# A projection's second pass with the rows of tiles 3 and 4 ahead of the old taps, and other moved steps

## The chip, the cores and the metric

The kernel runs on one NeuronCore of a Trainium2 chip. A core has five engines that take their instructions in order and meet by semaphores: TensorE (PE, matrix products), VectorE (DVE), ScalarE (ACT), GpSimd (POOL) and SyncE (SP), which here issues most of the DMAs. The metric is the device time of one execution in microseconds.

## The reference

One encoder layer, run on a prompt of 256 tokens and a sample of 2048, 2304 rows of 1024 channels in all, with the same weights. Cut to what matters:

```python
xn = rms_norm(x, norm1)
proj = xn @ w_in                       # hyena x0, x1, v | q | k | v
y_hy = hyena_mixer(...)                # short conv on x0, x1, v, then x0 * (filter * (x1 * v)) with an FFT
y_at = window_gqa(...)                 # |q - k| <= 128, q and k normed per head
h = x + concat(rms_norm(y_hy), rms_norm(y_at)) @ w_out
y = h + (silu(gate) * up) @ w_down     # gate, up = rms_norm(h, norm2) @ w_gate_up
```

All of it is fp32. A product of fp32 accuracy is made of three matmuls in a rounded fp32 format: each operand is split into a high part (a cast on ScalarE) and a low part (operand less high part, on VectorE), and high x high, low x high and high x low are summed. The function `triple` (lines 83 to 87) issues the three, so most of TensorE's rows carry the lines 85, 86 and 87.

## The kernel before

The program has three parts: `front` (input projection, the filter network and the long convolution's first half), `mixers` (convolution's end, attention, output projection) and `swiglu`. The change lies in `front` and at the seam of the other two.

`front` handles 18 tiles of 128 tokens, in 6 rounds over three groups of 6 tiles (`GT = 6`, `NG = 3`). Rounds 0 to 2 are the first pass, with 8 units each (the hyena's v and x1 columns). Rounds 3 to 5 are the second pass, with 10 units each (x0, q, k, v); there the rows come back from a copy in DRAM. A unit is 128 columns of `w_in`, and has two runs, c = 0 and c = 1, each over half of the group's tokens. A run is 24 matmuls, in two halves of 12 (`first_half`, `second_half`). Run 0 needs tiles 0 to 3 of the group, run 1 also tiles 4 and 5 (and, where the group "peeks", the first row of the next one, `turn(r, 6)`).

What each name does to the engines:

- `norm(n)`: the row sums of tile n on ScalarE (lines 1153 and 1155, the latter with another table of functions), the scaling on VectorE (1425). It belongs to the first pass.
- `turn(r, j)`: tile j of the round is transposed by TensorE (924, first pass) or read back (second pass), cast to `pr_xhi` in two halves by ScalarE (1188) and split to `pr_xlo` in two halves by VectorE (1451). VectorE counts the semaphore `x_low` by two per tile, and TensorE's runs wait for it. SP saves the tile before (559) and loads one ahead (551) in the same step.
- `weights(n)`: high and low part of a unit's weights (1161, 1429).
- `evict(r, i, c)`: the taps of the short convolution of a finished run: centre tap on ScalarE (1230), the two others on VectorE (1471, 1473), for the first pass followed by a product on GpSimd (761).
- the generator `side` holds the other work: the filter network with its sines (ScalarE 1280, 1292; VectorE 1518; GpSimd's preparation 767 to 772), the filter's transform in eighths (VectorE 1558, 1572), the transform of u (1346, 1576), and the products with the filter (TensorE's `pr_gen`, VectorE 1609, GpSimd 849 and 850, ScalarE casts, VectorE 1592 and 1596) and the return steps with the input `ir_z` (ScalarE 1396). `woven` advances it by one step at each `yield` of `course`.

`course` is one schedule that is run once per engine, with the engine's own pieces. So where it puts a call ahead of another, this holds on every engine that has a piece for it. On the way from one round to the next it has `turn(r, 2)`, the eviction of the last run, a side step, `turn(r, 3)`, a norm and a side step, ahead of unit 0. The second pass's scaling needs none of the norms, so there the norm is empty.

At the seam, the mixers' last tile t = 17 on GpSimd takes the low part of the hyena output, then that of the attention output (1974), then adds squares in pairs (1980, 1982), which TensorE sums with a matmul of ones (`am_score`, 2126). `scale_row(t)` scales the output row of a tile; the last two are called `close(0)` and `close(1)` and are handed to `swiglu`, whose GpSimd part calls them ahead of its first sums.

## Time and profile before

| | us |
|---|---|
| median of three runs | 2855.79 |
| lowest, highest | 2845.22, 2858.62 |
| profiled execution, its own time | 2853.9 |
| its span from the first to the last instruction | 2852.1 |
| PE busy | 2751.9 (96%) |
| DVE busy | 1869.4 (66%) |
| ACT busy | 1224.9 (43%) |
| POOL busy | 1031.1 (36%) |
| mean granted clock of TensorE | 0.991 |

A row of a timeline gives the start in us from the beginning of the span, the length, the engine (PE TensorE, DVE VectorE, ACT ScalarE, POOL GpSimd, SPq SyncE's queue), the line, the operation with output and inputs, and in brackets the idle time of that engine just ahead of it with what released it. `x4` says that four such instructions stand in a row; the length is then that of all four together. The granted clock is 1.00 at TensorE's full rate of 2.4 GHz and 0.50 at its lower level of 1.2 GHz.

### The profile page before, as it was taken

How to read it: one execution, taken by the hardware profiler on the slowest of the kernel's cores; microseconds unless marked ns; L12 is line 12 of the kernel's file. 1: busy time of each engine (PE TensorE's matmuls, PEld its weight loads, DVE VectorE, ACT ScalarE, POOL GpSimd, SP SyncE). 2: the span in 40 equal slices, each digit the busy share in tenths (PEclk: the TensorE clock that was granted, in tenths of full speed). 3: DMA queues.
4: the chain of work that ended last, by engine and by line, in shares of the span. 5: the costliest groups of instructions: out<-in, count | busy, mean ns of one | idle time of the engine just before them, and what ended most of it. 6: DMA issues, size and time to landing. Idle time of an engine off the chain costs nothing.

```text
span 2852.1 us, 38291 instructions
## 1 busy us (share of the span) xinstructions
PE 2751.9 (96%) x14280; PEld 2493.0 (87%) x14280; DVE 1869.4 (66%) x2575; ACT 1224.9 (43%) x1939; POOL 1031.1 (36%) x887
## 2 busy tenths in 40 slices
PE   6988899999998999998999999999999999999999
...
GB/s 207 129 263 176 282 256 235 266 239 174 225 266 211 105 140 127 118 114 180 86 96 102 88 81 71 234 73 92 86 93 78 78 195 105 64 78 67 71 67 67
DMA packets 391553, 405.30 MB, mean 142 GB/s; under 512 B 46271, under 2 KB 327231, under 8 KB 391080
## 3 DMA queue, kind: packets, MB, share of 16 engines
...
## 4 chain that ended last, share of the span: by engine, by line
PE 88%; DVE 5%; DMA 3%; issue 2%; ACT 2%; POOL 1%; SPq 0%; DVEq 0%; POOLq 0%; ACTq 0%
PE ff_banks L85 11%; PE ff_banks L87 11%; PE ff_banks L86 11%; PE ff_down L85 7%; PE ff_down L86 6%; PE ff_down L87 6%; PE pr_acc L85 4%; PE pr_acc L86 4%; PE pr_acc L87 4%; PE pr_gen L85 3%; PE pr_gen L87 3%; PE pr_gen L86 3%; PE am_mix L85 2%; PE am_mix L86 2%; PE am_mix L87 2%
## 5 line engine op out<-in xcount | busy, mean ns | idle before, releaser
L2756 POOL TENSOR_TENSOR ff_alo_raw<-ff_alo_raw,ff_silu 128x384 f32<-128x384 f32 x132 | 197.8, 1498 | 695.9 <-DVE ff_alo_raw L2980 622.1
L3002 DVE TENSOR_TENSOR ff_h<-ff_h,ff_down 128x512 f32<-128x512 f32 x396 | 264.5, 684 | 158.6 <-PE ff_down L87 155.7
L85 PE MATMUL pr_acc<-pr_xhi,pr_whi 128*128 128x386 f32 (+1 forms) x864 | 307.6, 356 | 20.1 <-DVE pr_xlo L1451 20.1
L85 PE MATMUL ff_banks<-ff_xhi,ff_ghi 128*128 128x384 f32 x924 | 313.0, 339 | 7.9 <-DVE ff_glo L2990 3.8
L85 PE MATMUL ff_down<-ff_dhi,ff_ahi 128*128 128x512 f32 x792 | 313.0, 395 | 3.5 <-issue 3.5
L86 PE MATMUL ff_down<-ff_dlo,ff_ahi 128*128 128x512 f32 x792 | 313.0, 395 | 0.0
L87 PE MATMUL ff_down<-ff_dhi,ff_alo 128*128 128x512 f32 x792 | 312.8, 395 | 0.0
L85 PE MATMUL ff_banks<-ff_xhi,ff_uhi 128*128 128x384 f32 x924 | 310.7, 336 | 1.1 <-DVE ff_ulo L2990 1.0
L87 PE MATMUL ff_banks<-ff_xhi,ff_glo 128*128 128x384 f32 x924 | 311.4, 337 | 0.0
L86 PE MATMUL ff_banks<-ff_xlo,ff_uhi 128*128 128x384 f32 x924 | 311.1, 337 | 0.0
L87 PE MATMUL ff_banks<-ff_xhi,ff_ulo 128*128 128x384 f32 x924 | 310.0, 336 | 0.0
L86 PE MATMUL ff_banks<-ff_xlo,ff_ghi 128*128 128x384 f32 x924 | 309.9, 335 | 0.0
L86 PE MATMUL pr_acc<-pr_xlo,pr_whi 128*128 128x386 f32 (+1 forms) x864 | 298.4, 345 | 0.0
L87 PE MATMUL pr_acc<-pr_xhi,pr_wlo 128*128 128x386 f32 (+1 forms) x864 | 297.2, 344 | 0.0
L2854 ACT CAST ff_ahi<-ff_alo_raw 128x384 fp32r<-128x384 f32 x132 | 67.8, 514 | 397.4 <-POOL ff_alo_raw L2756 397.2
L85 PEld LDWEIGHTS pr_acc<-pr_xhi,pr_whi 128*128 128x128 f32 x864 | 167.6, 194 | 32.0 <-DVE pr_xlo L1451 22.9
L85 PEld LDWEIGHTS ff_down<-ff_dhi,ff_ahi 128*128 128x128 f32 x792 | 148.5, 187 | 39.3 <-issue 4.4
L85 PEld LDWEIGHTS ff_banks<-ff_xhi,ff_ghi 128*128 128x128 f32 x924 | 173.4, 188 | 10.2 <-DVE ff_glo L2990 4.8
L87 PEld LDWEIGHTS ff_down<-ff_dhi,ff_alo 128*128 128x128 f32 x792 | 148.4, 187 | 36.3
L86 PEld LDWEIGHTS ff_down<-ff_dlo,ff_ahi 128*128 128x128 f32 x792 | 148.5, 188 | 34.6
L85 PEld LDWEIGHTS ff_banks<-ff_xhi,ff_uhi 128*128 128x128 f32 x924 | 173.4, 188 | 3.4 <-DVE ff_ulo L2990 2.0
L86 PEld LDWEIGHTS ff_banks<-ff_xlo,ff_uhi 128*128 128x128 f32 x924 | 173.4, 188 | 1.4
...
## 6 DMA issues: line engine op xcount, KB each, us to landing
...
```

The costliest lines, as they stand in the source:

```text
L85: pe.matmul(out, still[0], moving[0], start=start, stop=False)
L86: pe.matmul(out, still[0], moving[1], start=False, stop=False)
L87: return pe.matmul(out, still[1], moving[0], start=False, stop=stop)
L2756: pool.tensor_tensor(block(prod, c), block(prod, c), silu[c][:], ALU.mult).then_inc(tempered, 1)
L2854: act.copy(block(ahi, c), block(prod, c)).then_inc(a_high, 1)
L3002: dve.tensor_tensor(h[j][:, o], h[j][:, o], down(v), ALU.add).then_inc(added, 1)
```

## The change

Six things move; no instruction of arithmetic is added or taken away.

1. At the start `weights(0)` comes after `turn(0, 1)`. The 13 DMAs of constants on SP are issued in `turn(0, 1)`, behind the first tile's save, where before they came ahead of all turns. GpSimd's preparation of the third filter layer, which needs them, also waits for `x_low` 8.
2. In round 0, `turn(0, 3)` comes ahead of `norm(4)`, and in the first pass the norms of units 1 to 4 come behind the first half of run 1 instead of behind run 0's eviction, with a side step between the two places.
3. In the second pass `turn(r, 3)` comes ahead of the eviction of the last run. The two side steps between the rounds go: one behind run 0 of unit 0, the other behind the first half of run 1.
4. In unit 0 TensorE waits for a count of `x_low` that is one less (the first half of the last tile is enough) ahead of a run's first half, and for the full count ahead of the second half.
5. For the last tile, GpSimd's sums of squares come ahead of the low part of the attention output.
6. `scale_row(16)` is called in the mixers' last round, ahead of that round's store, not by `swiglu`.

```diff
@@ -241,3 +241,2 @@
         norm(1)
-        weights(0)
         turn(0, 0)
@@ -245,2 +244,3 @@
         turn(0, 1)
+        weights(0)
         norm(3)
@@ -249,10 +249,14 @@
             turn(r, 2)
+            if r >= NG:
+                turn(r, 3)
             if r:
                 evict(r - 1, units_of(r - 1) - 1, 1)
+            if 0 < r < NG:
                 yield
-            else:
+            if r < NG:
+                turn(r, 3)
+            if r == 0:
                 norm(GT - 2)
-            turn(r, 3)
             norm(GT * r + GT - 1)
-            if r:
+            if 0 < r < NG:
                 yield
@@ -276,4 +280,2 @@
                     turn(r, 6)
-                if 1 <= i <= 4 and r < ROUNDS - 1:
-                    norm(GT * r + GT + i)
                 if i == end and r < ROUNDS - 1:
@@ -281,2 +283,4 @@
                 yield
+                if i == 0 and r >= NG:
+                    yield
                 now[0] = event(r, i, 1)
@@ -284,2 +288,6 @@
                 first_half(r, i, 1)
+                if i == 0 and r >= NG:
+                    yield
+                if 1 <= i <= 4 and r < ROUNDS - 1:
+                    norm(GT * r + GT + i)
                 if i == end and r < ROUNDS - 1:
@@ -571,2 +579,11 @@
 
+        def constants():
+            for dst, src in ((cw[:], conv), (gq[:], gains), (ones[:], block_ones)):
+                sp.dma_start(dst, src).then_inc(consts, 16)
+            for dst, src in ((zt[:], z), (w1[:], f_w1), (w2[:], f_w2), (cols[:], f_cols), (w3in[0:64, 0], f_w3[:, 0:HY]),
+                             (w3in[0:64, 1], f_w3[:, HY:2 * HY]), (w3in[64:128, 1], f_w3[:, HY:2 * HY])):
+                sp.dma_start(dst, src).then_inc(f_consts, 16)
+            for s in range(2):
+                sp.dma_start(dec[:, s, :], decay[s]).then_inc(dec_in[s], 16)
+
         def turn(rd, j):
@@ -574,2 +591,4 @@
                 save_x(rd, j - 1)
+            if rd == 0 and j == 1:
+                constants()
             if 2 <= j < GT:
@@ -740,9 +759,2 @@
         bring_w(1)
-        for dst, src in ((cw[:], conv), (gq[:], gains), (ones[:], block_ones)):
-            sp.dma_start(dst, src).then_inc(consts, 16)
-        for dst, src in ((zt[:], z), (w1[:], f_w1), (w2[:], f_w2), (cols[:], f_cols), (w3in[0:64, 0], f_w3[:, 0:HY]),
-                         (w3in[0:64, 1], f_w3[:, HY:2 * HY]), (w3in[64:128, 1], f_w3[:, HY:2 * HY])):
-            sp.dma_start(dst, src).then_inc(f_consts, 16)
-        for s in range(2):
-            sp.dma_start(dec[:, s, :], decay[s]).then_inc(dec_in[s], 16)
         now = [0]
@@ -766,2 +778,3 @@
                     pool.wait_ge(f_consts, 16 * 7)
+                    pool.wait_ge(x_low, 8)
                     pool.tensor_tensor(w3[0:64, 0, :], w3in[0:64, 0, :], w3in[0:64, 1, :], ALU.add).then_inc(w3_sum, 1)
@@ -964,2 +977,5 @@
 
+        def rows_needed(rd, c):
+            return 2 * turn_number(rd, 4 if c == 0 else GT + peeks(rd))
+
         def half_chunk(rd, i, c, ks):
@@ -974,3 +990,3 @@
             if i == 0:
-                pe.wait_ge(x_low, 2 * turn_number(rd, 4 if c == 0 else GT + peeks(rd)))
+                pe.wait_ge(x_low, rows_needed(rd, c) - 1)
                 if rd and c == 0:
@@ -988,2 +1004,4 @@
         def second_half(rd, i, c):
+            if i == 0:
+                pe.wait_ge(x_low, rows_needed(rd, c))
             half_chunk(rd, i, c, range(4, KT)).then_inc(unit_done, 1)
@@ -1973,4 +1991,4 @@
                 pool.wait_ge(mixed, 4 * t - 4)
-            pool.tensor_tensor(ylo[:, t % 2, CT:KT], ao[:, t % 2], yhi[:, t % 2, CT:KT].bitcast(F32), ALU.subtract).then_inc(ya_low, 1)
-            pool.wait_ge(ya_low, t + 1)
+            if t < NTT - 1:
+                attention_rest(t)
             pool.wait_ge(squared, 2 * t + 2)
@@ -1983,2 +2001,8 @@
             pool.wait_ge(gathered, t + 1)
+            if t == NTT - 1:
+                attention_rest(t)
+
+        def attention_rest(t):
+            pool.tensor_tensor(ylo[:, t % 2, CT:KT], ao[:, t % 2], yhi[:, t % 2, CT:KT].bitcast(F32), ALU.subtract).then_inc(ya_low, 1)
+            pool.wait_ge(ya_low, t + 1)
 
@@ -2002,4 +2026,4 @@
 
-        def close(part):
-            scale_row(NTT - 2 + part)
+        def close():
+            scale_row(NTT - 1)
 
@@ -2016,3 +2040,3 @@
                 for i in range(units(n)):
-                    if i == 1 and 3 <= n <= NB:
+                    if i == 1 and 3 <= n:
                         scale_row(n - 3)
@@ -2763,3 +2787,2 @@
         def main(close):
-            close(0)
             sums(1)
@@ -2772,3 +2795,3 @@
                 if q == 0:
-                    close(1)
+                    close()
                 for n, b in enumerate((C11, C22, C21, C12)):
```

How this moves instructions is seen in the order of each engine. First VectorE at the change into group 3 (`pr_xlo` rows of tiles, 128x386 and 128x384 the taps, `fs_` the filter's transform), before:

```order
L1451 TENSOR_TENSOR pr_xlo<-pr_xs,pr_xhi 128x4x128 [waits pr_x_high] x4
L1471 SCALAR_TENSOR_TENSOR pr_cx<-pr_acc,pr_cw,pr_cx 128x386 [waits pr_centred]
L1473 SCALAR_TENSOR_TENSOR pr_cx<-pr_acc,pr_cw,pr_cx 128x386 [waits pr_tapped]
L1558 TENSOR_TENSOR fs_alo<-fs_a,fs_ahi 128x1024 [waits fi_a_high]
L1451 TENSOR_TENSOR pr_xlo<-pr_xs,pr_xhi 128x4x128 [waits pr_x_high] x2
L1558 TENSOR_TENSOR fs_alo<-fs_a,fs_ahi 128x1024 [waits fi_a_high]
L1572 COPY fs_out<-pr_gen 128x512 [waits fi_k_stored1,fi_eighths]
L1429 TENSOR_TENSOR pr_wlo<-pr_raw,pr_whi 128x1024 [waits pr_w_high]
L1451 TENSOR_TENSOR pr_xlo<-pr_xs,pr_xhi 128x4x128 [waits pr_x_high] x4
L1471 SCALAR_TENSOR_TENSOR pr_cx<-pr_acc,pr_cw,pr_cx 128x384 [waits pr_centred]
L1473 SCALAR_TENSOR_TENSOR pr_cx<-pr_acc,pr_cw,pr_cx 128x384 [waits pr_tapped]
L1451 TENSOR_TENSOR pr_xlo<-pr_xs,pr_xhi 128x4 [waits pr_x_high] x2
```

and after:

```order
L1469 TENSOR_TENSOR pr_xlo<-pr_xs,pr_xhi 128x4x128 [waits pr_x_high] x6
L1489 SCALAR_TENSOR_TENSOR pr_cx<-pr_acc,pr_cw,pr_cx 128x386 [waits pr_centred]
L1491 SCALAR_TENSOR_TENSOR pr_cx<-pr_acc,pr_cw,pr_cx 128x386 [waits pr_tapped]
L1447 TENSOR_TENSOR pr_wlo<-pr_raw,pr_whi 128x1024 [waits pr_w_high]
L1469 TENSOR_TENSOR pr_xlo<-pr_xs,pr_xhi 128x4x128 [waits pr_x_high] x2
L1576 TENSOR_TENSOR fs_alo<-fs_a,fs_ahi 128x1024 [waits fi_a_high]
L1469 TENSOR_TENSOR pr_xlo<-pr_xs,pr_xhi 128x4x128 [waits pr_x_high] x2
L1489 SCALAR_TENSOR_TENSOR pr_cx<-pr_acc,pr_cw,pr_cx 128x384 [waits pr_centred]
L1491 SCALAR_TENSOR_TENSOR pr_cx<-pr_acc,pr_cw,pr_cx 128x384 [waits pr_tapped]
L1469 TENSOR_TENSOR pr_xlo<-pr_xs,pr_xhi 128x4 [waits pr_x_high] x2
L1576 TENSOR_TENSOR fs_alo<-fs_a,fs_ahi 128x1024 [waits fi_a_high]
L1590 COPY fs_out<-pr_gen 128x512 [waits fi_k_stored1,fi_eighths]
```

Tile 3's two rows now stand with those of tiles 1 and 2 ahead of the taps, and the filter's low parts and the copy stand behind the weight's low part.

VectorE at the change into group 4 (`sp_pa`, `sp_pb` are the first products with the filter's transform), before:

```order
L1451 TENSOR_TENSOR pr_xlo<-pr_xs,pr_xhi 128x4x128 [waits pr_x_high] x2
L1471 SCALAR_TENSOR_TENSOR pr_cx<-pr_acc,pr_cw,pr_cx 128x384 [waits pr_centred]
L1473 SCALAR_TENSOR_TENSOR pr_cx<-pr_acc,pr_cw,pr_cx 128x384 [waits pr_tapped]
L1451 TENSOR_TENSOR pr_xlo<-pr_xs,pr_xhi 128x4x128 [waits pr_x_high] x2
L1609 TENSOR_TENSOR sp_pa<-sp_k,pr_gen 128x1024 [waits hy_h_spectral,hy_hk_in0]
L1609 TENSOR_TENSOR sp_pb<-sp_k,pr_gen 128x1024 [waits hy_h_spectral]
L1429 TENSOR_TENSOR pr_wlo<-pr_raw,pr_whi 128x1024 [waits pr_w_high]
L1451 TENSOR_TENSOR pr_xlo<-pr_xs,pr_xhi 128x4x128 [waits pr_x_high] x4
L1471 SCALAR_TENSOR_TENSOR pr_cx<-pr_acc,pr_cw,pr_cx 128x384 [waits pr_centred]
L1473 SCALAR_TENSOR_TENSOR pr_cx<-pr_acc,pr_cw,pr_cx 128x384 [waits pr_tapped]
L1451 TENSOR_TENSOR pr_xlo<-pr_xs,pr_xhi 128x4 [waits pr_x_high] x2
L1596 TENSOR_TENSOR sp_ylo<-sp_yf,sp_yhi 128x1024 [waits hy_y_high]
```

and after:

```order
L1469 TENSOR_TENSOR pr_xlo<-pr_xs,pr_xhi 128x4x128 [waits pr_x_high] x4
L1489 SCALAR_TENSOR_TENSOR pr_cx<-pr_acc,pr_cw,pr_cx 128x384 [waits pr_centred]
L1491 SCALAR_TENSOR_TENSOR pr_cx<-pr_acc,pr_cw,pr_cx 128x384 [waits pr_tapped]
L1447 TENSOR_TENSOR pr_wlo<-pr_raw,pr_whi 128x1024 [waits pr_w_high]
L1469 TENSOR_TENSOR pr_xlo<-pr_xs,pr_xhi 128x4x128 [waits pr_x_high] x4
L1489 SCALAR_TENSOR_TENSOR pr_cx<-pr_acc,pr_cw,pr_cx 128x384 [waits pr_centred]
L1491 SCALAR_TENSOR_TENSOR pr_cx<-pr_acc,pr_cw,pr_cx 128x384 [waits pr_tapped]
L1469 TENSOR_TENSOR pr_xlo<-pr_xs,pr_xhi 128x4 [waits pr_x_high] x2
L1627 TENSOR_TENSOR sp_pa<-sp_k,pr_gen 128x1024 [waits hy_h_spectral,hy_hk_in0]
L1627 TENSOR_TENSOR sp_pb<-sp_k,pr_gen 128x1024 [waits hy_h_spectral]
L1614 TENSOR_TENSOR sp_ylo<-sp_yf,sp_yhi 128x1024 [waits hy_y_high]
L1610 TENSOR_TENSOR sp_alo<-sp_a,sp_ahi 128x1024 [waits hy_ha_high]
```

The first pair of products went from ahead of the weight's low part to behind all rows of tiles 4 and 5 and the taps of run 0, next to the first low parts of `sp_y`.

ScalarE in round 0, unit 1 (`fi_feat` is the sine of the filter network, `pr_junk` the row sums of a norm), before:

```order
L1230 ACTIVATE pr_cx<-pr_acc,pr_cw 128x384 [waits pr_u_turned,pr_unit_done]
L1153 ACTIVATE pr_junk,pr_stat<-pr_xs 128x1024 [waits pr_scaled,pr_summed,pr_x_in4]
L1155 ACT_TABLE_LOAD
L1155 ACTIVATE pr_stat<-pr_stat,pr_eps 128x1 [waits pr_summed]
L1280 ACT_TABLE_LOAD
L1280 ACTIVATE fi_feat<-fi_arg 64x1152 [waits fi_wrapped0]
L1284 COPY fi_feat<-fi_feat 64x1 [waits fi_feat_zero,fi_waved]
L1292 CAST fi_fhi<-fi_feat 128x128 [waits fi_feat_first]
L1230 ACTIVATE pr_cx<-pr_acc,pr_cw 128x384 [waits pr_u_turned,pr_unit_done]
```

and after:

```order
L1248 ACTIVATE pr_cx<-pr_acc,pr_cw 128x384 [waits pr_u_turned,pr_unit_done]
L1298 ACTIVATE fi_feat<-fi_arg 64x1152 [waits fi_wrapped0]
L1302 COPY fi_feat<-fi_feat 64x1 [waits fi_feat_zero,fi_waved]
L1310 CAST fi_fhi<-fi_feat 128x128 [waits fi_feat_first]
L1171 ACTIVATE pr_junk,pr_stat<-pr_xs 128x1024 [waits pr_scaled,pr_summed,pr_x_in4]
L1173 ACT_TABLE_LOAD
L1173 ACTIVATE pr_stat<-pr_stat,pr_eps 128x1 [waits pr_summed]
L1248 ACTIVATE pr_cx<-pr_acc,pr_cw 128x384 [waits pr_u_turned,pr_unit_done]
```

The sine now stands ahead of the norm, and one load of a table is gone from between them.

## Rows read from the trace of the kernel before

**Rows 1.** The page's first part: engine busy us, share of the span, instructions.
```profile
PE 2751.9 (96%) x14280; PEld 2493.0 (87%) x14280; DVE 1869.4 (66%) x2575; ACT 1224.9 (43%) x1939; POOL 1031.1 (36%) x887
```

**Rows 2.** The waits of PE: engine, tile, line, releaser: us, times, longest.
```profile
PE pr_acc L85 <- DVE pr_xlo L1451: 20.1, 9, 4.4
```

**Rows 3.** Windows: us, busy by engine, granted clock, DMA share, GB/s.
```profile
433.00:443.00 10.00, 9.24 (x35) 8.71 (x36) 7.22 (x13) 4.32 (x10) 0.53 (x1) 0.69 1.12 342
...
566.00:581.00 15.00, 12.95 (x66) 11.58 (x66) 12.60 (x15) 4.45 (x7) 6.91 (x5) 1.00 1.10 323
```

**Rows 4.** Timelines into group 3: us, length, engine, line, operation, [idle before <- releaser].
```profile
426.39 2.48 DVE L1451 TENSOR_TENSOR pr_xlo<-pr_xs,pr_xhi 128x512 fp32r<-128x512 f32 x4
...
431.10 2.10 DVE L1451 TENSOR_TENSOR pr_xlo<-pr_xs,pr_xhi 128x512 fp32r<-128x512 f32 x2
...
433.25 0.69 PE L85 MATMUL pr_acc<-pr_xhi,pr_whi 128*128 128x386 f32 x1 [3.90 <-DVE pr_xlo L1451]
...
440.32 0.39 PE L85 MATMUL pr_gen<-fs_ahi,pr_g 128*128 128x512 f32 x1
...
442.70 0.44 PE L85 MATMUL pr_acc<-pr_xhi,pr_whi 128*128 128x386 f32 x1 [0.50 <-DVE pr_xlo L1451]
```

**Rows 5.** Timelines of ScalarE, VectorE and TensorE, change into group 4.
```profile
558.60 0.62 ACT L1346 CAST ur_uhi<-ur_us 128x512 fp32r<-128x512 f32 x1 [2.45 <-DMA ur_us<-u_rows]
...
566.85 4.69 DVE L1451 TENSOR_TENSOR pr_xlo<-pr_xs,pr_xhi 128x512 fp32r<-128x512 f32 x4
...
576.18 1.22 DVE L1609 TENSOR_TENSOR sp_pb<-sp_k,pr_gen 128x1024 f32<-128x1024 f32 x1
...
560.05 0.47 PE L85 MATMUL pr_gen<-ur_uhi,ur_ptable 128*128 128x512 f32 x1 [2.18 <-DVE ur_ulo L1576]
...
563.59 0.45 PE L85 MATMUL pr_acc<-pr_xhi,pr_whi 128*128 128x386 f32 x1 [0.56 <-DVE pr_xlo L1451]
...
567.95 0.39 PE L85 MATMUL pr_gen<-ur_uhi,ur_ptable 128*128 128x512 f32 x1
...
572.92 0.45 PE L85 MATMUL pr_acc<-pr_xhi,pr_whi 128*128 128x386 f32 x1 [2.05 <-DVE pr_xlo L1451]
...
577.25 0.39 PE L85 MATMUL pr_gen<-sp_ahi,pr_g 128*128 128x512 f32 x1
...
587.01 0.39 PE L85 MATMUL pr_gen<-sp_ahi,pr_g 128*128 128x512 f32 x1
```

**Rows 6.** Timelines of TensorE and ScalarE, change into group 5.
```profile
758.84 0.69 PE L85 MATMUL pr_acc<-pr_xhi,pr_whi 128*128 128x386 f32 x1 [4.44 <-DVE pr_xlo L1451]
...
765.29 0.40 PE L85 MATMUL pr_gen<-ir_zhi,ir_table 128*128 128x512 f32 x1
...
761.78 1.05 ACT L1396 CAST ir_zhi<-ir_z 128x1024 fp32r<-128x1024 f32 x1 [2.62 <-DMA ir_z<-z_dram]
```

**Rows 7.** Timelines of VectorE, GpSimd, TensorE and ScalarE at the start.
```profile
25.15 2.76 DVE L1451 TENSOR_TENSOR pr_xlo<-pr_xs,pr_xhi 128x512 fp32r<-128x512 f32 x2
...
24.11 2.23 POOL L768 TENSOR_TENSOR fi_h<-fi_w3in 64x512 f32<-64x512 f32 x1
...
27.97 0.69 PE L85 MATMUL pr_acc<-pr_xhi,pr_whi 128*128 128x386 f32 x1 [4.25 <-DVE pr_xlo L1451]
...
29.83 1.06 ACT L1153 ACTIVATE pr_junk<-pr_xs 128x1024 bf16<-128x1024 f32 x1 [4.27 <-DMA pr_xs<-x]
```

**Rows 8.** Timelines of ScalarE and TensorE in round 0, unit 1.
```profile
87.85 1.28 ACT L1280 ACT_TABLE_LOAD   x1
...
92.34 0.76 PE L85 MATMUL pr_gen<-fi_w3hi,fi_fhi 128*128 128x512 f32 x1 [3.62 <-DVE fi_flo L1518]
```

**Rows 9.** Timelines of GpSimd and TensorE at the mixers' last tile.
```profile
1289.83 3.35 POOL L1974 TENSOR_TENSOR am_ylo<-am_ao,am_yhi 128x512 fp32r<-128x512 f32 x1
...
1293.25 1.26 POOL L1980 TENSOR_TENSOR am_sq<-am_sq 128x512 f32<-128x512 f32 x1
...
1295.37 0.61 PE L2126 MATMUL am_score<-am_ones,am_sq 128*128 128x1 f32 x4 [3.74 <-POOL am_sq L1982]
```

## The prediction

> **What bounds the kernel now.** I read the shares of busy time first. TensorE is busy 2751.9 us of a span of 2852.1 [rows 1], so only 100.2 us of the span can be won by moving work, and the change takes no matmul away. Next I read what TensorE waits for: the largest releaser is VectorE's low part of the transposed rows, 20.1 us in 9 waits [rows 2], one or two at each group's start, and there the change works. Then I laid the timelines of TensorE, VectorE, ScalarE and GpSimd side by side at those starts, and at last the granted clock in windows around them. The clock matters as much as the idle time: the window 433 to 443, right behind a wait of 3.90, was granted 0.69, and the window 566 to 581, where the longest wait is 2.05, 1.00 [rows 3, 4, 5]. A run of 24 matmuls takes 440.32 - 433.25 = 7.07 us behind the long wait, 765.29 - 758.84 = 6.45 behind another of 4.44, and 567.95 - 563.59 = 4.36 where no long one precedes [rows 4 to 6]. So a long wait costs itself and up to 2.7 us more, for a stretch at the lower of the two clock levels, 1.2 GHz instead of 2.4.
>
> The profiled run took 2853.9 us (span 2852.1 and 1.8 around it), 1.9 under the median of the three runs, 2855.79, which reach from 2845.22 to 2858.62. My sum starts from 2853.9. About 0.5%, 14.3 us, is what a measurement of this kernel can tell from no change, and the three runs alone span 13.4.
>
> **Start.** Three edits meet: the low part of weight 0 goes behind the rows of tiles 0 and 1, the constants' 13 DMAs go behind the first saved tile, and with them GpSimd's five w3 operations (they now wait for the rows of tile 3). VectorE's pair for tile 3 took 2.76 us at 25.15, while GpSimd added at 24.11 for 2.23 [rows 7]; alone a pair is half of the 2.48 that four took at 426.39, so 1.24 [rows 4]. That is 1.5 us on the wait of TensorE that ends at 27.97 [rows 7]. The first run now starts on the first half of tile 3, one operation of 0.62 earlier, and the weight's low part (1.22 for that size, [rows 5]) is off VectorE's way ahead of it; ScalarE's chain of casts has no slack there and takes part of both back. Of 1.5 + 0.62 + 1.22 = 3.3 I keep 2.8: the first run starts at 25.2. On SP, tile 5's load stands behind a save that stood behind the constants, and its norm waited 4.27 us for it until 29.83 [rows 7]; 13 issues go from ahead of that load's save, so it comes earlier, by an estimated 4 us. Bounds: 1.5 (only the collision goes) to 4 (1.2 of tile 5's lead is kept in the second run as well). **+2.8**.
>
> **Round 0, norm order.** A norm stood ahead of the filter's sine on ScalarE, with a table loaded for it and another back, at 87.85 for 1.28; TensorE waited 3.62 for the filter's low part until 92.34 [rows 8]. With the norm behind the sine, its 1.06 (the same operation in [rows 7]), some 0.5 of small ones and two loads of 1.28 leave the path: the sine is 4.1 earlier. TensorE is ready at 92.34 - 3.62 = 88.7 and VectorE has taps to do first, so I take 89.5: 2.8 earlier. The next eviction on ScalarE and VectorE is then behind the norm, and gives about 1.1 back (an estimate: one norm operation); 1.7 is left, and 0.5 for the clock. Bounds 0 (it all comes back at the next eviction) to 5 (a shorter wait leaves the clock up; a half-rate stretch costs 2.7). **+2.2**.
>
> **Group 3.** Before, taps and the side step's filter work stood on VectorE between the pair of tile 2 (the last of the four from 426.39 for 2.48) and that of tile 3, which began at 431.10 and took 2.10 beside GpSimd's gate [rows 4]. Now six operations run straight from 426.39 at 0.62 each: the first half of tile 3 is ready at 426.39 + 5 x 0.62 = 429.5, and TensorE starts at 429.55 in place of 433.25, 3.7 earlier. But the 12 filter matmuls that filled TensorE between the two tiles are now behind the first run; such a step is 572.92 - 2.05 - 567.95 = 2.92 [rows 5]. Of the 3.7, 2.9 is given back later. The second run's wait of 0.50 at 442.70 goes [rows 4], and the wait of 3.90 becomes one of about 2.95, behind which I count half of a half-rate stretch's 2.7 (1.3) as won, less 0.3 for ScalarE's casts. 3.7 - 2.9 + 0.5 + 1.3 - 0.3 = **+2.3**, bounds 1.1 (clock as before, low taps late) to 3.8 (the whole half-rate stretch gone).
>
> **Group 4.** Here it goes the other way. ScalarE's cast of u waited 2.45 for a DMA until 558.60 [rows 5], and both tiles' casts stand behind it, in the old order and in the new. TensorE had 12 matmuls at 560.05 to fill the time up to 563.59 and now has none: it stands from 557.87 (560.05 - 2.18) to about 561.8, a wait of 3.9, as long as the two that a half-rate stretch followed. The step's two products on VectorE, which stood ahead of the rows of tiles 4 and 5 (566.85, [rows 5]), come behind them, so near 568.8. The product step at 577.25 then waits for a chain behind those products: GpSimd's two sums of 1.26 (its add of that size, [rows 9]), ScalarE's cast of 1.05 [rows 6], and four VectorE operations of 1.22 [rows 5]. I get 578.7 without a half-rate stretch, 579.7 with half of one, 581.5 with a full one; the long pair of 4.69 at 566.85 [rows 5] loses its neighbour on GpSimd and saves 2. Against 577.25 that is 1.45 to 4.25 lost, the vanished wait of 2.05 at 572.92 included; the middle is 2.85, and as the new wait is as long as those with a half-rate stretch behind them I go to **-3.3**, bounds -5.5 (a collision of 1.25 more) to -1.45.
>
> **Group 5.** TensorE starts at about 757.0 instead of 758.84 [rows 6], since tile 3's low part comes ahead of two taps and its second half is not waited for: three operations of some 0.62. Afterwards it is bound by the inverse step's input, whose cast waited 2.62 for a DMA at 761.78 [rows 6], and which no edit moves. With the 1.8 of the start and 0.5 for the clock I take **+2.3**; bounds 0.7 (the input decides) to 4 (the half-rate part of the 6.45 goes as well).
>
> **Mixers' end.** TensorE waited 3.74 at 1295.37 for the last tile's squares on GpSimd, behind operations of 3.35 and 1.26 [rows 9]. With the squares ahead of the 3.35 the sum comes up to 3.35 earlier, but the mix needs the low part too, and GpSimd's total is the same, so little is won: TensorE's sums of ones take 0.5. A scale row of the tile before leaves the front of the last phase's GpSimd work. **+0.5**, bounds 0 to 1.2. **Half-tile waits** in groups 1 and 2: an operation of 0.62 in two groups, but ScalarE's casts bind: **+0.3**, bounds 0 to 1.2.
>
> **Sum.** 2.8 + 2.2 + 2.3 - 3.3 + 2.3 + 0.5 + 0.3 = 7.1, so 2853.9 - 7.1 = 2846.8, forecast 2847. The bounds added with their signs: -2.2 to +17.75, so 2856.1 to 2836.1.
>
> **Two rules weighed.** The pair took 2.76 beside a GpSimd add [rows 7] and 1.24 alone [rows 4]. The Trainium skill, SBUF — State Buffer, "Who interferes with whom", says that a VectorE instruction with two SBUF inputs and a GpSimd one that reads SBUF exclude each other, the later one blocked until the other is done. The trace agrees, at 1.5 us a pair. By that rule the five w3 operations, moved and not removed, should do the same to whatever VectorE does next; this is rival C below, and by it the sum is 2852.
> The waits of 3.90 and 4.44 had half-rate matmuls behind them and waits up to 2.2 in group 4 had none. The Trainium skill, TensorE: Matmul & The Clock Gate, "Part 1: The HAM clock gate", has the throttled state as the default, released by activity, and the same kernel showing more or fewer half-rate matmuls each time it is measured. By it group 4's new wait of 3.9 would cost a full half-rate stretch in some executions and nothing in others; with the two bounds of that term the sum would be 2849 or 2845.
>
> **Rivals.**
> A, the sum: 2847, own range 2840 to 2853. Chance 0.58.
> B, clock: each of the shortened waits (start, round 0, groups 3 and 5) also leaves the clock up. That is 2.7 - 0.5 + 2.7 - 1.3 + 1.7 (group 5's bound) = 5.3 more than I counted, and group 4 keeps its clock, 1.85 more, with 1.2 at the start: 2847 - 8.4 = 2838.6. For it: 2.05 to 2.2 us waits with a window at 1.00 [rows 3, 5]. Against: the new waits at groups 3 and 4 are near 3 and 4. Chance 0.20, half of it past the bound of 0.5%.
> C, the waits only move: the five w3 operations (the 2.23 in [rows 7] is one) now start with TensorE's first run, against the norms and low parts of tiles 4 and 5, which TensorE's second run waits for; at 1.5 a collision, two take the start's 2.8 back, and round 0's taps take theirs. Left: 2.3 - 3.3 + 2.3 + 0.8 = 2.1, so 2852. For it: the second run's norm already was late at 29.83. Chance 0.14.
> D, slower: the product chain of group 4 stays late at every step. It has 2 x 1.26 + 1.05 + 4 x 1.22 = 8.45 us of work in a row, and TensorE goes from one product step to the next in 587.01 - 577.25 = 9.76 [rows 5]. It decides from 1.3 us more than that, one collision; with two of 1.5 in each of the 17 steps left, 1.7 x 17 = 29 us, 2876. Against: the step at 587.01 shows no wait. Chance 0.08, of which most is past the bound; that the change does nothing of what it says has no chance of its own, since the order of the instructions has moved.
>
> **Numbers.** Faster by over 0.5%: 0.10 from B, 0.06 from A and 0.01 from C by the scatter of runs, 0.17. Slower: 0.05 from D and 0.01 from C, 0.06. The rest, 0.77, is within 0.5%. The range has to hold A, C, most of B and the scatter of the runs: 2836 to 2860.
>
> **What would show it.** The first run at 25 to 26; the filter's matmuls at 90 rather than 92.34; group 3's first run near 429.6 with a wait near 3; in group 4 a wait near 3.9 ahead of the first run where there was 0.56, and the product step of 577.25 later than before by 1 to 4 us, relative to the group's start; at group 5 a first wait under 4.44. Wrong would be: TensorE idle time (span less busy) not lower by 3 us or more; a wait of over 1 us at each product step (D); or GpSimd's w3 operations beside a VectorE pair of over 2 us ahead of the second run (C).

## The result

The changed kernel took 2839.57 us, median of 9 runs (2835.42 to 2846.35), the kernel before 2855.79 (2845.22 to 2858.62, 9 runs). The medians are 16.2 us apart. The ratio over all runs is 0.9949, 95% interval 0.9936 to 0.9961: 14.6 us faster (11 to 18), at the bound of 0.5%. The forecast was 2847, its range 2836 to 2860.

The profiled run has a span of 2835.1. The page's first part, as in [rows 1], and the waits of TensorE, as in [rows 2]:

```profile
PE 2748.3 (97%) x14280; PEld 2490.5 (88%) x14280; DVE 1865.6 (66%) x2575; ACT 1223.8 (43%) x1937; POOL 1030.9 (36%) x887
```

```profile
PE pr_acc L85 <- DVE pr_xlo L1469: 13.7, 8, 2.9
```

The span less TensorE's busy time fell from 100.2 to 86.8 us, 13.4, and its busy time by 3.6 (fewer matmuls at half rate). These make the 17.0 between the two spans. But the waits for tile rows, on which the prediction was built, give only 20.1 - 13.7 = 6.4 of it. Where the rest went is seen when matmuls of the same number are laid beside each other in the two traces. The lead of the changed kernel is, on the old kernel's time axis, in this pair of traces and in a second pair (the same two kernels profiled again, see the first experiment):

| old time, us | place | lead, us | since the row above | second pair: lead | since the row above |
|---|---|---|---|---|---|
| 28 | first run of round 0 | 3.1 | +3.1 | 3.6 | +3.6 |
| 46 | end of round 0, unit 0 | 5.6 | +2.5 | 3.7 | 0.0 |
| 83 | sine waves done | 4.2 | -1.4 | 6.1 | +2.4 |
| 103 | round 0, filter begins | 7.7 | +3.5 | 8.0 | +1.8 |
| 188 | round 1, unit 0 | 6.2 | -1.4 | 8.7 | +0.8 |
| 325 | into round 2 | 15.0 | **+8.8** | 16.3 | **+7.6** |
| 446 | group 3 through | 17.4 | +2.4 | 19.1 | +2.8 |
| 580 | group 4 through | 14.6 | -2.8 | 16.7 | -2.4 |
| 769 | group 5 through | 15.7 | +1.1 | 17.8 | +1.1 |
| 890 | attention begins | 14.5 | -1.2 | 15.9 | -1.9 |
| 1333 | mixers' end through | 17.0 | +2.5 | 15.8 | -0.1 |

Only the step of 188 to 325 is far above what the two pairs differ by, and no term of the prediction over 0.3 stands there. The timelines of TensorE and VectorE there show what went. Before, round 1, unit 1 (TensorE first):

```profile
207.68 0.47 PE L85 MATMUL pr_gen<-fi_hhi,fi_table 128*128 128x512 f32 x1 [1.96 <-issue]
```

```profile
204.55 1.89 DVE L1425 SCALAR_TENSOR_TENSOR pr_xs<-pr_xs,pr_stat,pr_gbc 128x1024 f32<-128x1024 f32 x1
206.36 1.21 DVE L1537 TENSOR_TENSOR fi_hlo<-fi_h,fi_hhi 128x1024 fp32r<-128x1024 f32 x1
```

and VectorE of the changed kernel at the same place:

```profile
197.92 1.22 DVE L1555 TENSOR_TENSOR fi_hlo<-fi_h,fi_hhi 128x1024 fp32r<-128x1024 f32 x1
...
200.66 1.28 DVE L1443 SCALAR_TENSOR_TENSOR pr_xs<-pr_xs,pr_stat,pr_gbc 128x1024 f32<-128x1024 f32 x1
```

The profile names no releaser for the wait of 1.96 ("issue"), but the matmuls need `fi_hlo`, and that ended at 207.57, 0.1 us before they began. It stood behind a tile's scaling, line 1425, which took 1.89 there beside GpSimd's gate. In the changed kernel the scaling stands behind it, takes 1.28, and TensorE does not wait. The kernel before has four waits without a releaser on `pr_gen`, 6.3 us in all, but only three of them are for `fi_hlo`: 1.96, 1.02 and 1.96 at 207, 226 and 245, 4.9 us. The fourth is for the inverse step in group 5, and the changed kernel still has it, as its only one:

```profile
831.90 0.47 PE L85 MATMUL pr_gen<-ir_zhi,ir_table 128*128 128x512 f32 x1 [1.39 <-issue]
```

```profile
817.33 0.47 PE L85 MATMUL pr_gen<-ir_zhi,ir_table 128*128 128x512 f32 x1 [1.72 <-issue]
```

Behind the fourth scaling of round 1 the wait for `fi_hlo`, here with its releaser named, fell from 2.20 to 1.08. Together that is 6.1 us of waiting. Most of the rest of the step is the clock: the 15 us behind the last of these waits were granted 0.89 before and 1.00 in the changed kernel:

```profile
277.00:292.00 15.00, 13.65 (x63) 12.03 (x63) 3.47 (x5) 2.58 (x4) 3.53 (x3) 0.89 0.48 141
```

```profile
265.00:280.00 15.00, 11.77 (x63) 10.58 (x61) 4.23 (x5) 3.62 (x5) 3.52 (x3) 1.00 0.59 169
```

The 63 matmuls took 13.65 us and then 11.77.

The rows that answer to [rows 4 to 9], TensorE of the changed kernel, in order of time:

```profile
24.88 0.69 PE L85 MATMUL pr_acc<-pr_xhi,pr_whi 128*128 128x386 f32 x1 [1.93 <-DVE pr_xlo L1469]
...
86.48 0.47 PE L85 MATMUL pr_gen<-fi_w3hi,fi_fhi 128*128 128x512 f32 x1 [1.47 <-DVE fi_flo L1536]
...
414.33 0.60 PE L85 MATMUL pr_acc<-pr_xhi,pr_whi 128*128 128x386 f32 x1 [2.92 <-DVE pr_xlo L1469]
...
423.87 0.45 PE L85 MATMUL pr_acc<-pr_xhi,pr_whi 128*128 128x386 f32 x1 [0.43 <-DVE pr_xlo L1469]
...
543.12 0.46 PE L85 MATMUL pr_acc<-pr_xhi,pr_whi 128*128 128x386 f32 x1 [2.65 <-DVE pr_xlo L1469]
...
561.00 0.57 PE L85 MATMUL pr_gen<-sp_ahi,pr_g 128*128 128x512 f32 x1 [2.08 <-DVE sp_pa L1627]
...
742.43 0.69 PE L85 MATMUL pr_acc<-pr_xhi,pr_whi 128*128 128x386 f32 x1 [2.65 <-DVE pr_xlo L1469]
...
751.63 0.47 PE L85 MATMUL pr_gen<-ir_zhi,ir_table 128*128 128x512 f32 x1 [1.18 <-DVE ir_zlo L1635]
...
1279.22 0.61 PE L2150 MATMUL am_score<-am_ones,am_sq 128*128 128x1 f32 x4 [2.13 <-POOL am_sq L2000]
```

Ahead of the first runs 4.25 became 1.93, 3.90 became 2.92 and 4.44 became 2.65, and the filter's wait of 3.62 became 1.47. At group 4 the wait of 0.56 became 2.65, and a new wait of 2.08 for the products' first operation came. When the same kernel was profiled again, group 4's was 3.76:

```profile
543.73 0.69 PE L85 MATMUL pr_acc<-pr_xhi,pr_whi 128*128 128x386 f32 x1 [3.76 <-DVE pr_xlo L1469]
```

The granted clock in windows (us, busy of the engines, clock, DMA share, GB/s) around groups 3, 4 and 5:

```profile
414.00:424.00 10.00, 9.25 (x40) 8.47 (x41) 9.10 (x15) 7.03 (x14) 2.47 (x2) 0.83 1.08 299
543.00:560.00 17.00, 15.80 (x72) 14.48 (x72) 11.63 (x18) 6.80 (x12) 3.12 (x3) 0.90 0.94 277
742.00:752.00 10.00, 8.40 (x38) 8.07 (x39) 8.55 (x14) 6.18 (x10) 0.00 (x0) 0.83 0.69 181
```

Behind group 3's shorter wait the clock was 0.83 where it had been 0.69, and group 4, at 1.00 before, is at 0.90 [rows 3]. That the shorter wait made group 3's difference is not shown. Here are norms_only, a kernel of the experiments below with the old wait of 3.89, and pass2_only, with the new one of 2.92:

```profile
422.50:432.50 10.00, 9.28 (x41) 8.73 (x42) 8.01 (x14) 5.43 (x11) 0.53 (x1) 0.83 1.12 349
```

```profile
426.00:436.00 10.00, 9.56 (x35) 8.90 (x36) 7.90 (x11) 5.80 (x12) 2.46 (x2) 0.68 1.06 298
```

Over all traces with the wait of 3.9 the 10 us behind it were granted 0.69 to 0.72 three times and 0.83 four times, over those with 2.92, 0.68 or 0.69 twice and 0.83 or 0.84 four times.

### The profile page after: what moved, and what is told of

It is laid out like the page before. It is cut to its first block, busy times and chain, and to the rows that moved or that the text cites. A ratio compares the mean times of both kernels' runs of the same rounds, so it can differ in the third digit from the quotient of the medians.

```text
span 2835.1 us, 38290 instructions
## 1 busy us (share of the span) xinstructions
PE 2748.3 (97%) x14280; PEld 2490.5 (88%) x14280; DVE 1865.6 (66%) x2575; ACT 1223.8 (43%) x1937; POOL 1030.9 (36%) x887
## 4 chain that ended last, share of the span: by engine, by line
PE 89%; DVE 4%; DMA 2%; ACT 2%; issue 2%; POOL 1%; SPq 0%; DVEq 0%; ACTq 0%; POOLq 0%
PE ff_banks L85 11%; PE ff_banks L87 11%; PE ff_banks L86 11%; PE ff_down L85 7%; PE ff_down L86 7%; PE ff_down L87 7%; PE pr_acc L85 4%; PE pr_acc L86 4%; PE pr_acc L87 4%; PE pr_gen L85 3%; PE pr_gen L87 3%; PE pr_gen L86 3%; PE am_mix L85 2%; PE am_mix L86 2%; PE am_mix L87 2%
## 5 line engine op out<-in xcount | busy, mean ns | idle before, releaser
L85 PE MATMUL pr_acc<-pr_xhi,pr_whi 128*128 128x386 f32 (+1 forms) x864 | 306.4, 355 | 13.7 <-DVE pr_xlo L1469 13.7
L85 PEld LDWEIGHTS pr_acc<-pr_xhi,pr_whi 128*128 128x128 f32 x864 | 166.6, 193 | 25.4 <-DVE pr_xlo L1469 15.9
```

The source lines that it names most:

```text
L85: pe.matmul(out, still[0], moving[0], start=start, stop=False)
```

## Experiments

Ratios are to the kernel before, measured beside each; a gain is 1 less the ratio, times 2855.8 us. The profile of each kernel is of one of its executions. Those of norms_round1 and vector_norms_late took 2853.37 and 2853.09 us, where the medians are 2846.92 and 2848.24, so these traces are read for single waits and steps and not for totals.

| kernel | ratio, 95% interval | gain, us |
|---|---|---|
| changed kernel | 0.9949 (0.9936 to 0.9961) | 14.6 |
| start_only | 0.9987 (0.9978 to 0.9995) | 3.7 |
| norms_only | 0.9950 (0.9937 to 0.9963) | 14.3 |
| norms_round1 | 0.9967 (0.9956 to 0.9979) | 9.4 |
| vector_norms_late | 0.9977 (0.9967 to 0.9988) | 6.6 |
| start_norms | 0.9951 (0.9938 to 0.9963) | 14.0 |
| pass2_only | 1.0000 (0.9992 to 1.0008) | 0.0 |
| g4_filled | 0.9938 (0.9921 to 0.9954) | 17.7 |
| rows_first_filled | 0.9943 (0.9927 to 0.9959) | 16.3 |
| old_end | 0.9961 (0.9947 to 0.9976) | 11.1 |
| w3_no_wait | 0.9947 (0.9934 to 0.9959) | 15.1 |

**Is it chance or order?** Both kernels were profiled once more, unchanged.

> The kernel before, unchanged, profiled a second time. In the first pair of traces the changed kernel gains 8.8 us between 188 and 324 us of the old time axis (rounds 1 and 2), which no step of the prediction names: three waits of TensorE without a releaser (1.96, 1.02, 1.96 us) and a filter wait are gone, and one stretch at the lower clock. Theory chance: these waits come and go between executions of one program, so this profile shows other ones (the sum of TensorE's waits without releaser on pr_gen differs from 6.3 us by 2 or more, or they stand at other places). Theory order: they belong to the old order of instructions and stand at the same matmuls again, 6.3 us in 4 waits. Both expect a total within 2845 to 2859.

> The changed kernel, unchanged, profiled a second time. Theory chance: waits without releaser on pr_gen appear again in some number (2 to 6 us in total), rounds 1 and 2 are not 8.8 us shorter than before but 3 to 6. Theory order: again at most one such wait in all (1.7 us), and rounds 1 and 2 are shorter by 7 to 10 us. Both expect 2835 to 2847.

They took 2854.61 and 2838.95 us. The waits of TensorE on `pr_gen` without a releaser, the kernel before again, then the changed kernel again:

```profile
PE pr_gen L85 <- issue: 6.0, 5, 2.0
```

```profile
PE pr_gen L85 <- issue: 1.9, 1, 1.9
```

In both traces of before the three waits for `fi_hlo` stand at the same matmuls with the same lengths, and in neither of the changed kernel is one of them (the second has a wait of 0.98 at 208, for a DMA of `fi_table`). The step of 188 to 325 is 7.6 us in the second pair. The waits belong to the order. What does change between two executions is where the clock falls, and some waits behind a DMA: over the whole span the two traces of before drift by 0.7 us from each other, those of the changed kernel by 2.0. A step of some 2 us is therefore read from no single pair of traces.

**The start alone.** The start's edits of the change, put into the kernel before:

```diff
-        weights(0)
         turn(0, 0)
         norm(2)
         turn(0, 1)
+        weights(0)
...
+            if rd == 0 and j == 1:
+                constants()
...
+                    pool.wait_ge(x_low, 8)
```

> The kernel before with the edits of the start alone (weights(0) behind the first two turns, constants behind the first save, GpSimd's w3 operations behind x_low 8). By the prediction the first run of TensorE starts at 25 instead of 27.97 and 2.8 us stay to the end: about 2853, ratio 0.9990. Rival theory (all of it is the clock): the wait at 40 us gets shorter, the clock stays up, 5.7 us stay: ratio 0.998. Rival theory (later waits take it back): the first run is earlier, and by 170 us nothing is left: ratio 1.000.

Measured 3.7 us (1.4 to 6.3); the first run starts at 25.48 there. The forecast of 2.8 and the rival at 5.7 are both inside; the one by which nothing stays is just outside.

**The norms alone.**

```diff
-                if 1 <= i <= 4 and r < ROUNDS - 1:
-                    norm(GT * r + GT + i)
...
                 first_half(r, i, 1)
+                if 1 <= i <= 4 and r < ROUNDS - 1:
+                    norm(GT * r + GT + i)
```

> The kernel before with the new place of norms 7 to 10 of each group alone. By the prediction the filter's matmuls that waited 3.62 us at 92.34 come 2.8 earlier and 2.2 us stay: about 2853.5, ratio 0.9992. Rival theory, order: this edit also removes the waits without releaser in rounds 1 and 2 and gains 8 us or more there: ratio 0.996 to 0.997. Rival theory, nothing: the taps behind the norm give all of it back.

14.3 us (10.6 to 18.0): as much as the whole change. Then the same move in round 1 only:

```diff
-                if 1 <= i <= 4 and r < ROUNDS - 1:
+                if 1 <= i <= 4 and r < ROUNDS - 1 and r != 1:
                     norm(GT * r + GT + i)
...
                 first_half(r, i, 1)
+                if 1 <= i <= 4 and r == 1:
+                    norm(GT * r + GT + i)
```

> The kernel before with the norms of round 1 (units 1 to 4) alone moved behind run 1's first half; round 0 stays. The trace of norms_only shows that in round 1 the norm's scaling on VectorE (1.28, up to 1.88) stood ahead of the filter's low part fi_hlo, for which TensorE waited 1.96, 1.02, 1.96 and 2.20 us. Theory queue: these four waits go, 5 to 6 us, and about half of the shorter stretches at the lower clock with them: 6 to 8 us, ratio 0.9972 to 0.9980, and the waits of round 0 (3.62 at 92) stay. Rival theory, sine: round 0's sine and the clock behind it make the gain, so this kernel gains under 3 us: 0.999 or more.

9.4 us (6.0 to 12.6). None of the three waits without a releaser is left in round 1, the named one for `fi_hlo` is 1.08, and the wait of 3.6 for `fi_flo` in round 0 stays. The theory that the sine makes all of the gain falls. Round 0's norms were never moved alone; the difference of the two kernels, 4.9 us, has an interval of about 5 to either side. Last, in round 1 VectorE's part of the norm alone is late, and ScalarE's stays in its place (a flag that only VectorE's call of `course` sets):

```diff
-                if 1 <= i <= 4 and r < ROUNDS - 1:
+                if 1 <= i <= 4 and r < ROUNDS - 1 and not (late and r == 1):
                     norm(GT * r + GT + i)
...
                 first_half(r, i, 1)
+                if 1 <= i <= 4 and late and r == 1:
+                    norm(GT * r + GT + i)
```

> The kernel before; in round 1 the norm's two operations on VectorE (reciprocal and scaling) alone stand behind run 1's first half, ScalarE's part stays in the old place. Theory queue on VectorE: fi_hlo waited behind the scaling, so the waits of 1.96, 1.02, 1.96 and most of 2.20 us go as in norms_round1: ratio 0.9965 to 0.998. Rival theory, ScalarE: its row sums and table load ahead of the copies of the filter's outputs make the waits, they stay, ratio 0.999 to 1.000.

6.6 us (3.4 to 9.4). VectorE of this kernel at the place shown above:

```profile
205.26 1.22 DVE L1539 TENSOR_TENSOR fi_hlo<-fi_h,fi_hhi 128x1024 fp32r<-128x1024 f32 x1
...
208.00 1.28 DVE L1427 SCALAR_TENSOR_TENSOR pr_xs<-pr_xs,pr_stat,pr_gbc 128x1024 f32<-128x1024 f32 x1
```

The three waits are gone here too. So the place of one VectorE operation of 1.28 us (and of the reciprocal of 0.16 ahead of it), four times, is what makes the waits, and by the middle of the intervals it makes most of round 1's gain; ScalarE alone can't be what makes them. All traces agree on the place: with any form of the new norm order (ten traces, the changed kernel's included) the step of 188 to 325 is 7.1 to 9.5 us over the first trace of before, with the old order (before_again, start_only, pass2_only) it is 0.1, 0.1 and 1.2. Whether ScalarE's move adds the other 2.8 us is not told apart by these intervals.

**Start and norms together.** Both edits above, nothing else.

> The kernel before with the start's edits and all the norms' new places together, and nothing of the second pass, the half-tile waits or the mixers' end. If the terms add up, 0.9987 x 0.995 = 0.9937, so 2839: as fast as the changed kernel or up to 3 us faster. Theory second pass pays (prediction: groups 3 to 5, end and half tiles +2.1): this one is 2 us slower than the changed kernel (0.9957 of before). Rival theory second pass costs: it is 1 to 5 us faster than the changed kernel (0.993 or less of before).

14.0 us (10.6 to 17.7), not the 18 that the two add up to, and equal to the changed kernel within the intervals. Those of the two single edits are wide enough (start 1.4 to 6.3, norms 10.6 to 18.0) that a loss of 4 is not shown. One place where a lead could end is the start of round 1. The wait of TensorE there is for `pr_ust`, in the kernel before, the kernel before again, start_only, norms_only, this kernel and the changed kernel:

```profile
174.82 1.94 PE L924 MATMUL pr_turned<-pr_ident,pr_xs 128*128 128x128 f32 x8 [4.01 <-ACT pr_ust L1203]
```

```profile
175.92 1.30 PE L924 MATMUL pr_turned<-pr_ident,pr_xs 128*128 128x128 f32 x5 [5.98 <-ACT pr_ust L1203]
```

```profile
171.51 1.94 PE L929 MATMUL pr_turned<-pr_ident,pr_xs 128*128 128x128 f32 x8 [6.47 <-ACT pr_ust L1208]
```

```profile
174.04 1.30 PE L924 MATMUL pr_turned<-pr_ident,pr_xs 128*128 128x128 f32 x5 [5.57 <-ACT pr_ust L1203]
```

```profile
170.51 1.73 PE L929 MATMUL pr_turned<-pr_ident,pr_xs 128*128 128x128 f32 x7 [4.76 <-ACT pr_ust L1208]
```

```profile
169.18 1.94 PE L937 MATMUL pr_turned<-pr_ident,pr_xs 128*128 128x128 f32 x8 [6.62 <-ACT pr_ust L1221]
```

On ScalarE a copy stands ahead that waits until a store of the filter to DRAM has landed (kernel before, kernel before again, then changed):

```profile
172.28 0.59 ACT L1298 COPY fi_out<-pr_gen 128x512 f32<-128x512 f32 x1 [2.08 <-DMA f_dram<-fi_out]
```

```profile
173.38 0.58 ACT L1298 COPY fi_out<-pr_gen 128x512 f32<-128x512 f32 x1 [4.02 <-DMA f_dram<-fi_out]
```

```profile
166.64 0.59 ACT L1316 COPY fi_out<-pr_gen 128x512 f32<-128x512 f32 x1 [4.08 <-DMA f_dram<-fi_out]
```

The wait does not grow with the lead: the same kernel has 4.01 once and 5.98 once with no lead at all, norms_round1 has 7.17 with none, and start_norms, 5 us ahead, has 4.76. So it differs by 2 us and more between executions whatever the order, and where the sum's 4 us went, if they went, stays open.

**The second pass alone**, with the half-tile waits:

```diff
             turn(r, 2)
+            if r >= NG:
+                turn(r, 3)
             if r:
                 evict(r - 1, units_of(r - 1) - 1, 1)
...
+                if i == 0 and r >= NG:
+                    yield
...
-                pe.wait_ge(x_low, 2 * turn_number(rd, 4 if c == 0 else GT + peeks(rd)))
+                pe.wait_ge(x_low, rows_needed(rd, c) - 1)
...
         def second_half(rd, i, c):
+            if i == 0:
+                pe.wait_ge(x_low, rows_needed(rd, c))
```

> The kernel before with the new order between the rounds of the second pass and the half-tile waits alone. By the prediction +2.3 at group 3, -3.3 at group 4, +2.3 at group 5, +0.3: 1.6 us faster, ratio 0.9994. Rival theory (clock at the group starts decides): 5 us faster, 0.998. Rival theory (the product chain and the later steps take it back): ratio 1.000 to 1.001.

Nothing, within 2.3 us either way. The forecast of 1.6 is inside, 5 is not.

**Group 4 with its side steps back.** In the changed kernel:

```diff
-            if 0 < r < NG:
+            if 0 < r < NG or r == 4:
                 yield
...
-            if 0 < r < NG:
+            if 0 < r < NG or r == 4:
                 yield
...
-                if i == 0 and r >= NG:
+                if i == 0 and r >= NG and r != 4:
                     yield
...
-                if i == 0 and r >= NG:
+                if i == 0 and r >= NG and r != 4:
                     yield
```

> The changed kernel with both side steps of round 4 back between the eviction and unit 0, the rows of tiles 2 and 3 still ahead of the old taps; groups 3 and 5 as in the changed kernel. Theory filler: TensorE's 12 matmuls stand in the wait for tile 3 again and the products on VectorE stand ahead of the rows of tiles 4 and 5, so group 4 costs nothing: 3 us faster than the changed kernel, 2836 to 2837, ratio 0.9938 of before. Rival theory casts: ScalarE's cast behind the late DMA binds group 4 in either order, and the time is that of the changed kernel within 1 us.

TensorE at group 4:

```profile
543.13 0.47 PE L85 MATMUL pr_gen<-ur_uhi,ur_ptable 128*128 128x512 f32 x1 [2.79 <-DVE ur_ulo L1594]
...
556.03 0.45 PE L85 MATMUL pr_acc<-pr_xhi,pr_whi 128*128 128x386 f32 x1 [1.32 <-DVE pr_xlo L1469]
```

The 12 matmuls stand ahead of the first run again, which follows them without a wait, and the wait of 2.08 for `sp_pa` is gone. Matmuls of the same number have a lead of 2.3 us over the changed kernel when group 4 is through; at the end of the span 0.5 of it is left. All traces side by side say it better than this pair. From 446 to 580 of the old axis the five traces with moved side steps lose 2.1, 2.8, 3.9, 4.3 and 5.5 us against the first trace of before, those with the side steps in the old place between a gain of 0.4 and a loss of 0.7. So moving them costs 2 to 5.5 us in group 4. The totals, 2837.47 and 2839.57, point the same way, but their intervals overlap: it has the lowest median of all, and is not shown to be faster than the changed kernel.

**The filler in all groups.** Here no side step of rounds 3 to 5 is moved, only the rows come first:

```diff
-            if 0 < r < NG:
+            if r:
                 yield
...
-            if 0 < r < NG:
+            if r:
                 yield
...
-                if i == 0 and r >= NG:
-                    yield
...
-                if i == 0 and r >= NG:
-                    yield
```

> The changed kernel with both side steps back between the rounds in all of rounds 3 to 5, so that of the second pass's edit only the rows of tiles 2 and 3 ahead of the old taps is left. Theory filler: at group 3 the 12 filter matmuls fill TensorE's wait again and the first run starts 3.7 us earlier than in the kernel before with under 0.5 us of waiting ahead of it, at full clock: 2.9 us and a share of a half-rate stretch better than g4_filled, ratio 0.9925 to 0.993 of before. Rival theory: the filter's low parts, now behind all six row operations on VectorE, are late for the next filter step, and the gain over g4_filled is under 1 us.

16.3 us (11.7 to 20.8) against the 20 to 21.4 forecast for the filler. Both theories saw half. TensorE at group 3, first and second run, g4_filled, then this kernel:

```profile
414.20 0.69 PE L85 MATMUL pr_acc<-pr_xhi,pr_whi 128*128 128x386 f32 x1 [2.92 <-DVE pr_xlo L1469]
...
423.76 0.44 PE L85 MATMUL pr_acc<-pr_xhi,pr_whi 128*128 128x386 f32 x1 [0.43 <-DVE pr_xlo L1469]
```

```profile
426.77 0.69 PE L85 MATMUL pr_acc<-pr_xhi,pr_whi 128*128 128x386 f32 x1 [4.05 <-DVE pr_xlo L1465]
```

The wait of 2.92 ahead of the first run is 0.17 here. But VectorE now has two low parts of the filter and a copy ahead of the weight's low part and of tiles 4 and 5, and the second run waits 4.05 for these. Through group 3 g4_filled gained 2.2 us and this kernel 1.2, a difference that one pair of traces does not tell from drift, and the timed intervals overlap. So in group 4 moving the side steps costs, and in group 3 it is not shown to pay.

**The mixers' end as before** in the changed kernel, `attention_rest(t)` ahead of the squares again and `close(0)` at the swiglu's start:

```diff
-            if t < NTT - 1:
-                attention_rest(t)
+            attention_rest(t)
...
         def main(close):
+            close(0)
             sums(1)
```

> The changed kernel with the mixers' end as before (squares of the last tile behind the attention's low part, scale_row(16) at swiglu's start). By the prediction the new end gains 0.5 us, bounds 0 to 1.2: this kernel is at 0.9951 of before. In the pair of traces the step from 1295 to 1332 us of the old axis gained 1.5 to 2.5; by that it is at 0.9955 to 0.9958. Below 0.9945 would say that the new end costs.

11.1 us (6.9 to 15.1) against 14.6: a difference of 3.5, but the two intervals overlap widely, so the new end is not shown to pay in the timed runs. GpSimd and VectorE of the changed kernel at the last tile, beside [rows 9], and VectorE of the kernel before:

```profile
1272.35 2.59 POOL L1985 TENSOR_TENSOR am_ylo<-am_yp,am_yhi 128x512 fp32r<-128x512 f32 x1 [0.18 <-POOL am_ao L1978]
1275.02 3.35 POOL L1998 TENSOR_TENSOR am_sq<-am_sq 128x512 f32<-128x512 f32 x1
1278.44 0.72 POOL L2000 TENSOR_TENSOR am_sq<-am_sq 128x256 f32<-128x256 f32 x1
1279.24 1.27 POOL L2006 TENSOR_TENSOR am_ylo<-am_ao,am_yhi 128x512 fp32r<-128x512 f32 x1
...
1271.48 2.31 DVE L3013 TENSOR_TENSOR ff_glo<-ff_glo_raw,ff_ghi 128x1536 fp32r<-128x1536 f32 x1
...
1274.96 2.28 DVE L3013 TENSOR_TENSOR ff_glo<-ff_glo_raw,ff_ghi 128x2048 fp32r<-128x2048 f32 x1
```

```profile
1289.78 2.28 DVE L2990 TENSOR_TENSOR ff_glo<-ff_glo_raw,ff_ghi 128x2048 fp32r<-128x2048 f32 x1
```

**GpSimd's w3 operations without their wait:**

```diff
                     pool.wait_ge(f_consts, 16 * 7)
-                    pool.wait_ge(x_low, 8)
```

> The changed kernel without the wait of GpSimd's w3 operations for x_low 8; they start when their constants are there. Rival C of the prediction (moved collisions take the start's gain back) expects either order to collide, so no difference, 0.995. The prediction's start term expects the collision on the pair of tile 3 to come back where the constants land in time: up to 1.5 us slower than the changed kernel, and the VectorE pair ahead of the first run at over 2 us. If the constants, issued later, land behind the first run anyway, there is no difference and the wait does nothing.

No difference that the runs can tell (11.7 to 18.8 us against 11 to 18); a loss of 1.5 us, as the start's term expects, would be within the noise. VectorE without and with the wait:

```profile
24.00 2.37 DVE L1468 TENSOR_TENSOR pr_xlo<-pr_xs,pr_xhi 128x512 fp32r<-128x512 f32 x2 [1.91 <-ACT pr_xhi L1205]
...
26.48 2.11 DVE L1442 SCALAR_TENSOR_TENSOR pr_xs<-pr_xs,pr_stat,pr_gbc 128x1024 f32<-128x1024 f32 x1
```

```profile
24.13 1.29 DVE L1469 TENSOR_TENSOR pr_xlo<-pr_xs,pr_xhi 128x512 fp32r<-128x512 f32 x2 [1.90 <-ACT pr_xhi L1206]
...
26.22 1.72 DVE L1443 SCALAR_TENSOR_TENSOR pr_xs<-pr_xs,pr_stat,pr_gbc 128x1024 f32<-128x1024 f32 x1
```

The pair is longer by 1.1 without the wait, yet the first run starts at 24.75, no later, because it needs only the pair's first half. With the half-tile start the wait buys nothing there; whether it does without it was not run.

## Why the prediction was right, and where not

The side and the range held; the size was half of what came, 7.1 us summed against 14.6. The measured 2839.57 is just below the range of 2840 to 2853 that the sum alone allowed for, and in the full range because that was made wide enough for rival B. That it lies within 1 us of B's 2838.6 is luck: B wanted 8.4 us from a clock that stays up, and TensorE's busy time, in which that would stand, fell by 3.6, about half of it in round 1, where B had no term.

- **Start, +2.8.** Right: 24.88 for the first run against 25.2 said, and 3.7 us alone (1.4 to 6.3). The pair of tile 3 took 1.29 in place of 2.76. Tile 5's load came 2.2 earlier and not 4 (its norm began at 27.67). The constants are 12 DMAs, not 13; nothing hangs on it.
- **Norm order, +2.2.** This is the step that failed, in its size, with its bound of 5 far off: 14.3 us (10.6 to 18.0). It was worked out for one place, the sine in unit 1 of round 0, where the matmuls' wait fell from 3.62 to 1.47. But the edit moves the norm in units 1 to 4 of both rounds 0 and 1, eight times. In round 1 the scaling stood ahead of `fi_hlo` on VectorE, and the move in that round is worth 9.4 us (6.0 to 12.6). I had read the waits by releaser and taken the largest named one; 4.9 of the 6.3 us put down to "issue" were for an operand behind another operation in VectorE's queue.
- **Group 3, +2.3.** 2.4 and 2.8 in the two pairs: start 3.9 us earlier relative to the steps ahead (15.0 to 18.9), the wait 2.92 where 2.95 was said, the 12 matmuls given back later. But 1.3 of the term was for a clock that the shorter wait keeps up, and that is not borne out: behind either length of wait the clock was 0.69 in some traces and 0.83 in others. Where the clock was the same, 0.68 to 0.72, pass2_only and w3_no_wait kept 0.9 and 0.4.
- **Group 4, -3.3.** -2.8 and -2.4 in the two pairs, and 2 to 5.5 lost over all traces with moved side steps. The wait ahead of the first run was 2.65 in the first trace, but 3.76 to 4.20 in the four others with this order, as the 3.9 said. The products' chain was late by 2.08 once and not after: rival D fell.
- **Group 5, +2.3.** The start came as said; the matmuls of the inverse step then waited 1.18 for their input, which the bound of 0.7 stood for. 1.1 was gained in both pairs. Up to 890 the lead fell again, by 1.2 and 1.9, but so it did in start_norms and start_only, which have no edit there (1.1 and 1.3).
- **Second pass in all.** 0.0 (within 2.3) against 1.6 forecast with the half tiles. The title's part of the change is worth nothing that could be measured.
- **Mixers' end, +0.5.** Not settled. TensorE's wait fell by 1.6 (3.74 to 2.13), but a new one of 0.8 for `am_mix` came behind it; the swiglu's first waits fell by 1.2 in all. From 1290 to 1333 that made 2.5 in the first pair and 0.9 in the second, and the timed runs' 3.5 is within their noise. The 3.35 that I took off the squares' path was not bound to the low part: the first of the squares' adds now takes 3.35, where it stands now, and the low part 1.27.
- **Rival C** was half right: the scaling of tile 4 took 1.72 and that of tile 5 1.49 beside the w3 operations where 1.28 is the length alone. TensorE waited 1.04 for tile 5's until 30.92, so at most 0.2 us of it came onto its path, not the 2.8 that C counted.
- **The rule on exclusive access** (the Trainium skill, SBUF — State Buffer, "Who interferes with whom") agrees with the pair at 2.37 and 1.29 above, and it also bears on the scaling of round 1, 1.89 beside GpSimd's gate and 1.28 behind it.
- **The rule on the clock** (the Trainium skill, TensorE: Matmul & The Clock Gate, "Part 1: The HAM clock gate") agrees in that traces of one program, or of programs with the same wait, differ in where the lower clock stands. Waits of 2.65 and 2.92 were followed by part of a run at half rate, and one of 3.9 by a window at 0.69 or at 0.83, so no price of a wait in clock can be read from one trace, as the prediction did with its 2.7.

Open: what share of round 1's 9.4 us is ScalarE's move (6.6 came from VectorE's alone), what round 0's norms give alone, and what of the mixers' end is the squares and what the moved scale row, which were never run apart.
